# Gate-up biases as a 128-row fp32 table, chunk scores as 64x64 blocks, modulation rows turned by products with 36 moving columns

## What is computed

```
sh1, sc1, gt1, sh2, sc2, gt2 = split(silu(c) @ w_mod + b_mod)      # one row for the prompt, 8 for the samples
h  = rmsnorm(x) * (1 + sc1) + sh1
aq, af, ai, ag, bq, bk, bv, ga, gb = split(h @ w_in)
# HGRN2 branch, chunks of 64 tokens: inside a chunk
a = where(causal, einsum('bntha,bnsha->bnhts', q_dec, k_dec), 0)
# ... differential attention, merge, w_out, residual, second norm: h2
e1..e4 = top4(h2 @ w_router + b_router)                            # of 32 experts
gu = xb @ w_gate_up[e] + b_gate_up[e]                              # glu, lin = halves of 1024 columns
y  = ((clip(lin, -7, 7) + 1) * min(glu, 7) * sigmoid(1.702 * glu)) @ w_down[e] + b_down[e]
```

## Time and profile before

| | |
|---|---|
| runs | 1260.77, 1265.24, 1265.37 us |
| median | 1265.24 us |
| span of the profiled execution | 1258.5 us |
| TensorE products busy | 1102.0 us, 88% of the span |
| weight loads of TensorE / VectorE / ScalarE / GpSimd busy | 456.6 / 588.2 / 230.7 / 68.5 us |
| DMA | 485.30 MB, mean 386 GB/s |

### The profile page before, as it was taken

How to read it: one execution, slowest core, us unless ns; L and a number is a source line. 1 busy time by engine, 2 the same in 40 slices (tenths; PEclk the granted TensorE clock), 3 DMA queues, 4 the chain that set the end, 5 groups by cost and what they waited for, 6 DMA issues and landing times.

```text
span 1258.5 us, 23992 instructions
## 1 busy us (share of the span) xinstructions
PE 1102.0 (88%) x9856; PEld 456.6 (36%) x9856; DVE 588.2 (47%) x1166; ACT 230.7 (18%) x420; POOL 68.5 (5%) x126
## 2 busy tenths in 40 slices
PE   8999999999988697996887979999966995667996
PEld 4776777785322131321222322333211331112332
DVE  3536744444654252563353544666532552332654
ACT  3002510141311110220111211112100211100212
POOL 0312020250100000000000000000000000000000
PEclk9999999999989897998798999999988998888999
DMA  9979994599899999999999999999999999999995
GB/s 342 312 245 347 317 339 154 187 384 366 284 428 429 426 429 426 429 425 429 426 428 428 428 426 393 409 424 427 428 427 428 427 426 430 424 431 425 428 428 236
DMA packets 67619, 485.30 MB, mean 386 GB/s; under 512 B 6421, under 2 KB 29450, under 8 KB 40762
## 3 DMA queue, kind: packets, MB, share of 16 engines
q1 hardware_dynamic: 59312, 461.07, 88.9%
q0 software_dynamic: 7104, 19.65, 4.9%
q10 hardware_dynamic: 1130, 3.51, 0.8%
HBM read 479.47 MB, written 4.72 MB: 385 GB/s over the span
## 4 chain that ended last, share of the span: by engine, by line
DMA 45%; PE 27%; DVE 1%; issue 0%; DVEq 0%; ACT 0%; ACTq 0%
DMA big<-in_w_down 26%; PE PB L1247 13%; DMA big<-in_w_gate_up 13%; PE PB L1274 7%; DMA hTG<-in_w_down 5%; PE PB L1214 2%; PE PB L1201 2%; PE PB L1206 1%; PE PB L1229 1%; PE PB L1221 1%; PE PB L1240 0%; PE PB L1186 0%; PE PB L1232 0%; DVE big L1623 0%; DVE big L1620 0%
## 5 line engine op out<-in xcount | busy, mean ns | idle before, releaser
L1247 PE MATMUL PB<-big,cst 128*32 128x512 f32 x2768 | 355.0, 657 | 109.2 <-DMA big<-in_w_gate_up 109.2
L2189 DVE TENSOR_TENSOR tok<-PB,cst 32x512 f32<-32x512 f32 x188 | 129.1, 687 | 261.7 <-ACT cst L1554 259.8
L1247 PEld LDWEIGHTS PB<-big,cst 128*32 128x32 f32 x2768 | 89.0, 115 | 345.2 <-issue 181.1
L1274 PE MATMUL PB<-big,cst 128*32 128x512 f32 x1408 | 166.6, 602 | 12.8 <-DMA big<-in_w_down 12.7
L2165 DVE TENSOR_SCALAR mod<-PB 64x256 f32<-64x256 f32 x96 | 41.0, 427 | 209.1 <-PE PB L1247 208.4
L756 PE MATMUL PB<-hTG,big 128*128 128x264 f32 x576 | 136.5, 391 | 0.4 <-DVE hTG L1617 0.4
L756 PEld LDWEIGHTS PB<-hTG,big 128*128 128x128 f32 x576 | 106.9, 190 | 27.3 <-issue 10.8
L1544 ACT ACTIVATE mod<-PB 64x256 f32<-64x256 f32 x96 | 36.1, 376 | 422.3 <-PE PB L1247 421.7
L1274 PEld LDWEIGHTS PB<-big,cst 128*32 128x32 f32 x1408 | 39.2, 110 | 96.8 <-issue 65.8
L1201 PE MATMUL PB<-wide,att 128*32 128x256 f32 x784 | 57.9, 415 | 5.1 <-DVE att L2159 4.9
L1554 ACT ACTIVATE cst<-PB 128x512 f32<-128x512 f32 x48 | 28.7, 597 | 178.2 <-PE PB L1274 178.2
(11 more groups left out here) (378 smaller groups left out, 970.9 us busy)
## 6 DMA issues: line engine op xcount, KB each, us to landing
big<-in_w_gate_up SPq DMA_DIRECT2D x115, 2048.0 KB, 31.0
big<-in_w_down SPq DMA_DIRECT2D x57, 2048.0 KB, 23.9
hTG<-in_w_gate_up SPq DMA_DIRECT2D x13, 2048.0 KB, 37.1
big<-in_w_mod SPq DMA_DIRECT2D x24, 1024.0 KB, 7.5
big<-in_w_in SPq DMA_DIRECT2D x22, 1024.0 KB, 9.2
hTG<-in_w_down SPq DMA_DIRECT2D x6, 2048.0 KB, 24.0
wide<-in_cache_k POOLq DMA_DIRECT2D x16, 256.0 KB, 6.8
big<-in_w_out SPq DMA_DIRECT2D x4, 1024.0 KB, 10.5
```

The lines of the kernel that those rows point to most:

```text
L1247: mm = pe.matmul(GU[32 * j:32 * j + 32, :], mo["xT"][:, (2 * u + r) * M:(2 * u + r + 1) * M], groups(w[:, r * 2 * D:(r + 1) * 2 * D])[:, j ...
L1274: mm = pe.matmul(DN[32 * j:32 * j + 32, :], mo["actT"][:, (4 * u + r) * M:(4 * u + r + 1) * M], w[:, r * D + half * 512:r * D + (half + 1) ...
L2189: mm = dve.tensor_tensor(mo["y"][rows, :], DN[rows, :], mo["y_part"][other, :], ALU.add)
```

## The change

- biases becomes 128 rows of 512 fp32: rows 32j+e hold group j of expert e, filled by eight DMAs of the GpSimd queue with runs of 128 elements (512 bytes). VectorE adds 1 to rows 64 to 127 and signals biases_ready; the bf16 split, sel, and GpSimd's copy for it are gone.
- In `gate_up` each of the four bias products has a column of the fp32 identity, repeated 32 times, as stationary operand and the whole table as moving one. They stand ahead of the wait for xT_ready.
- Filler and clearing products read repeated zero rows in place of the biases tile; its clearing at the start is gone.
- `chunk_scores` makes two 64x64 products per head instead of one of 128x128.
- `first_cols` and `mod_cols` use an ordinary product of the same 128x128 stationary tile with the 36 useful columns of the identity; VectorE's reads follow.

```diff
@@ -189,8 +189,7 @@
         G = hTG[:, KC * T:KC * T + 2 * D].rearrange("p (s n) -> p s n", s=2)
         att_even = sb("att", [P, 2, 384])
         tok = sb("tok", [P, W])
-        biases = sb("biases", [96, 2 * D], BF16)
-        sel = sb("sel", [96, E], BF16)
+        biases = sb("biases", [P, 512])
         zeros_mask = sb("zeros", [P, P + NCH * E], BF16)
         zeros = zeros_mask[0:96, NCH * E:]
         small = sb("small", [P, 672])
@@ -210,6 +209,7 @@
             return cst[0:rows, at:at + w]
 
         ident = C("ident")
+        vector_rows = ident.rearrange("p (j r) -> p j r", j=4)[:, :, 0:9]
 
         def late_tile(i, n=H * T):
             return late[:, i * H * T:i * H * T + n]
@@ -262,8 +262,6 @@
         SH1p = late[:, 4 * SLOT:4 * SLOT + 256].rearrange("p (k r) -> p k r", k=KC)
         r4_rows = late[:, 4 * SLOT + 256:4 * SLOT + 768]
         b4_cols = late[:, 4 * SLOT + 768:4 * SLOT + 768 + 4 * 9].rearrange("p (j r) -> p j r", j=4)
-        bias_f = gates[0:E, 0:3 * D]
-        bias_t = gates[0:E, 3 * D:4 * D]
         wr = sb("wr", [P, KC, E])
         wrA = C("scan")[:, 0:KC * E].rearrange("p (k e) -> p k e", k=KC)
         br = sb("br", [P, E])
@@ -518,7 +516,11 @@
                 pool.dma_start(mod[32 * j:32 * j + 9, 1:3, :], src).then_inc(S("bmod_loaded"), 16)
             for i, n in enumerate(("lam_q1", "lam_k1", "lam_q2", "lam_k2")):
                 pool.dma_start(lamv[:, i, :], bass.AP(a[n].tensor, 0, [[0, P], [1, 64]])).then_inc(S("lam_loaded"), 16)
-            pool.dma_start(bias_f[:, 0:2 * D], a["b_gate_up"][0]).then_inc(S("bias_loaded"), 16)
+            for j in range(4):
+                src = a["b_gate_up"][0].rearrange("e (t u h j c) -> e t j h u c", t=2, u=2, h=2, j=2)[:, j // 2, j % 2]
+                dst = biases[32 * j:32 * j + 32, :].rearrange("e (h u c) -> e h u c", h=2, u=2)
+                for h in range(2):
+                    pool.dma_start(dst[:, h], src[:, h]).then_inc(S("bias_loaded"), 16)
             for j in range(4):
                 g = a["g_post_mix"] if j < 2 else a["g_post_ffn"]
                 src = bass.AP(g.tensor, (j % 2) * 512, [[0, 32], [1, 512]])
@@ -609,8 +611,6 @@
             for j in range(4):
                 pool.dma_start(own_cols_of(x_spill, j), own_rows(sx1, j)).then_inc(S("x_spilled"), 16)
 
-            pool.wait_ge(S("cst_loaded"), 16)
-            pool.tensor_copy(sel[:, :], C("onehot_e", 96)).then_inc(S("sel_ready"), 1)
             pool.wait_ge(S("h2_ready"), NCH)
             pool.wait_ge(S("x_spilled"), 16 * 4)
             pool.wait_ge(S("aux_full"), AUX["rt1"] + 1)
@@ -638,10 +638,14 @@
             def tr(out, in_, n=P):
                 return pe.transpose(out, in_, ident[0:n, 0:n])
 
+            def no_rows(n):
+
+                return zeros[:, 0:n // 4].unsqueeze(1).to_broadcast([96, 4, n // 4])
+
             def idle_products(n):
 
                 for _ in range(n):
-                    pe.matmul(PB[3][:, :], zeros[:, :], biases[:, 0:512], start=True, stop=True)
+                    pe.matmul(PB[3][:, :], zeros[:, :], no_rows(512), start=True, stop=True)
 
             pe.wait_ge(S("zeros_ready"), 1)
             idle_products(6)
@@ -687,7 +691,8 @@
                 pe.wait_ge(S("mod_free" if kind == 0 else "sc_rows"), 1)
                 bank = begin(name)
                 for q in range(2):
-                    mm = tr(bank[:, q * P:(q + 1) * P], mod[:, 0, kind * 256 + q * P:kind * 256 + (q + 1) * P])
+                    mm = pe.matmul(bank[:, q * 36:(q + 1) * 36], mod[:, 0, kind * 256 + q * P:kind * 256 + (q + 1) * P],
+                                   vector_rows, start=True, stop=True)
                 full(mm)
 
             def first_unit_shift():
@@ -731,7 +736,8 @@
                 pe.wait_ge(S("mod_free"), g + 1)
                 bank = begin(name)
                 for q in range(4):
-                    mm = tr(bank[:, q * P:(q + 1) * P], mod[:, g, q * P:(q + 1) * P])
+                    mm = pe.matmul(bank[:, q * 36:(q + 1) * 36], mod[:, g, q * P:(q + 1) * P], vector_rows,
+                                   start=True, stop=True)
                 full(mm)
 
             def proj_bank(name):
@@ -807,8 +813,11 @@
                 bank = begin(f"as{c}")
                 pe.wait_ge(S("hg_qk"), 1)
                 for h in range(H):
-                    mm = pe.matmul(bank[:, h * P:(h + 1) * P], KD[:, h, c * P:(c + 1) * P],
-                                   AQ[:, h, c * P:(c + 1) * P], start=True, stop=True)
+                    for i in range(2):
+                        cols = slice(c * P + i * CHUNK, c * P + (i + 1) * CHUNK)
+                        at = h * P + i * CHUNK
+                        mm = pe.matmul(bank[CHUNK * i:CHUNK * (i + 1), at:at + CHUNK], KD[:, h, cols], AQ[:, h, cols],
+                                       start=True, stop=True)
                 full(mm)
 
             def chunk_update(c):
@@ -1122,12 +1131,12 @@
                 full(pe.matmul(bank[:, 0:E], lparts[:, c, :], C("onehot_e"), start=True, stop=True))
 
             def zero(bank, n):
-                pe.matmul(bank[:, 0:n], zeros[:, :], biases[:, 0:n], start=True, stop=False)
+                pe.matmul(bank[:, 0:n], zeros[:, :], no_rows(n), start=True, stop=False)
 
             def add_zeros(n):
 
                 for _ in range(n):
-                    pe.matmul(acc(0, 0), zeros[:, :], biases[:, 0:512], start=False, stop=False)
+                    pe.matmul(acc(0, 0), zeros[:, :], no_rows(512), start=False, stop=False)
 
             out_samples()
             out_rows(0, 0, 0, 2)
@@ -1234,11 +1243,11 @@
                 mm.then_inc(S("gates_turned"), 1)
 
             def gate_up(e, b):
-                    pe.wait_ge(S("xT_ready"), b + 1)
                     pe.wait_ge(S("pgT_ready"), b + 1)
                     for j in range(4):
-                        pe.matmul(GU[32 * j:32 * j + 32, :], sel[:, e:e + 1].to_broadcast([96, M]), groups(biases[:, :])[:, j // 2, j % 2],
-                                  start=True, stop=False)
+                        pe.matmul(GU[32 * j:32 * j + 32, :], ident[:, 32 * j + e:32 * j + e + 1].to_broadcast([P, M]),
+                                  biases[:, :], start=True, stop=False)
+                    pe.wait_ge(S("xT_ready"), b + 1)
                     for u in range(4):
                         pe.wait_ge(*unit_landed(e * NU + u))
                         w = unit_slot(e * NU + u)
@@ -1282,7 +1291,7 @@
             gather()
             pe.wait_ge(S("aux_free"), AUX["rt1"] + 1)
             zero(ACC2, 256)
-            pe.wait_ge(S("sel_ready"), 3)
+            pe.wait_ge(S("biases_ready"), 1)
             blocks_of_first = pe.alloc_register("blocks_of_first")
             pe.reg_mov(blocks_of_first, 1)
             pe.wait_ge(S("samples_act"), 7)
@@ -1626,7 +1635,7 @@
                 do(dve.tensor_copy(out, in_), sem)
 
             do(dve.memset(zeros[:, :], 0.0))
-            do(dve.memset(biases[:, 0:512], 0.0), "zeros_ready")
+            dve.nop().then_inc(S("zeros_ready"), 1)
             do(dve.memset(small[:, :], 0.0))
             do(dve.memset(eps[:, :], EPS), "ssq_zero")
             do(dve.memset(cT[:, :, :], 0.0))
@@ -1667,13 +1676,13 @@
 
             def scale_cols(A, b4, kind, gains):
 
-                src = b4.rearrange("p (q j r) -> p j q r", q=4, j=4)[:, 2 * kind:2 * kind + 2, :, 0:9]
+                src = b4[:, 0:144].rearrange("p (q j r) -> p j q r", q=4, j=4)[:, 2 * kind:2 * kind + 2]
                 for j in range(2):
                     g = VT[:, gains + 4 * j:gains + 4 * j + 4].unsqueeze(2).to_broadcast([P, 4, 9])
                     stt(A[:, 4 * j:4 * j + 4, :], src[:, j], 1.0, g, ALU.add, ALU.mult)
 
             def shift_cols(SH, b4, kind):
-                src = b4.rearrange("p (q j r) -> p j q r", q=4, j=4)[:, 2 * kind:2 * kind + 2, :, 0:9]
+                src = b4[:, 0:144].rearrange("p (q j r) -> p j q r", q=4, j=4)[:, 2 * kind:2 * kind + 2]
                 for j in range(2):
                     copy(SH[:, 4 * j:4 * j + 4, :], src[:, j])
 
@@ -1681,7 +1690,7 @@
                 dve.nop().then_inc(S("aux_free"), 1)
 
             def by_group(b):
-                return b[:, 0:256].rearrange("p (q j r) -> p q j r", q=2, j=4)[:, :, :, 0:9]
+                return b[:, 0:72].rearrange("p (q j r) -> p q j r", q=2, j=4)
 
             dve.wait_ge(S("mod_used"), 4)
             copy(mod[:, 0, 256:512], PB[4][:, 0:256], "sc_rows")
@@ -1728,15 +1737,8 @@
                 do(dve.tensor_reduce(sv("lam", i, i + 1), lamv[:, 2 * i, :], AX, ALU.add))
             dve.nop().then_inc(S("lam_dots"), 1)
 
-            dve.wait_ge(S("bias_loaded"), 16)
-            ts(bias_f[:, D:2 * D], bias_f[:, D:2 * D], 1.0, None, ALU.add)
-            for i in range(2):
-                cols = slice(i * D, (i + 1) * D)
-                for part in range(3):
-                    copy(biases[32 * part:32 * part + 32, cols], bias_f[:, cols])
```

(5 more changed lines are left out.)

## The result

| | before | after |
|---|---|---|
| median, us | 1263.05 (20 runs, 1259.15 to 1329.51) | 1266.91 (20 runs, 1264.84 to 1273.43) |
| ratio after/before, 95% interval | | 1.0044 (1.0029 to 1.006) |
| span of the profiled execution, us | 1258.5 | 1263.4 |
| that execution's own time, us | not given | 1265.09 |

The ratio leaves the disturbed run of 1329.51 us out; on 1263.05 us it is +5.6 us (3.7 to 7.6), and the means of the 19 other runs before and the 20 after, 1262.7 and 1268.2 us, lie 5.5 us apart. The kernel became slower, but by less than the forecast's 7.8 us; 1266.91 us is, rounded, the lowest value of the range, and the ratio lies inside the 0.5% that counted as no change, with the interval across that border.

A forecast was written before the change was run, and what follows sets the result against it. TensorE's product list was taken to bound the kernel to about 340 us, the expert weight stream after that. Front stage +1.0 and expert stage +6.8 us on 1265.2 gave 1273.0 us, range 1267 to 1279.

The forecast's parts named there:

- Price of the group: Four bias products of each expert block: fp32 group 0.86 us for 0.22, so 0.64 us more TensorE time per block.
- rival 3: Expert blocks: bias products run two after two, not abreast; a group takes 1.7 us, 1285 us in all; chance 0.06.
- First block: Start of the expert stage: fp32 group starts 0.43 us sooner but lasts 0.64 us longer, +0.2 us on the path.
- Stall: Late slot release at 786.31 us, where the weight stream waits for TensorE: two more costly blocks, +1.3 us.
- Three experts: Two-block experts behind the 786.31 us release: period 30.30 us against 29.4 of DMA, 0.9 us each, +2.7 us (0 to 3.9).
- rival 1: Expert stage: queued weights cover the three experts, the tail pays only its last two groups; +3.8 us, 1269 us; chance 0.30.
- Tail: Last blocks, from 1157.11 us to the end: six bias groups less 1.2 us of waiting, +2.6 us (1.3 to 3.8).
- Part 2: Front stage, modulation rows by 36 columns: turned tiles go from 0.12 to 0.20 us, twelve tiles, +1.0 us (-1.0 to 1.4).
- Part 3: Front stage, chunk scores as 16 half-size instructions for 8: no change, ends for two calls -0.7 and +1.2 us.
- Part 4: Bias preparation at the start: fewer VectorE instructions, eight GpSimd DMA issues for one; priced at 0, ends -1.5 and +3.8 us.
- rival 4: Front stage: GpSimd's 3.8 us of later issues come through to the cached key pages; 1277 us; chance 0.06.
- The sum's base: Starting time of the whole-kernel sum: 1265.2 us, the median of runs, taken to stand 6.7 us over the profiled 1258.5 us span.

The follow-up runs named there:

- r1 to r3: Changed kernel with bf16 bias table, fp32 bias group issued twice in experts 15-19; 1-14 and 20-27; or 28-31: ratios 1.0086, 1.0037, 1.0068 to the kernel before.

## Why the prediction was right or wrong

**Bound and mechanism: right.** Two regimes, a stall at 780 to 790 us, a stream with 0.4 us to spare per two-block expert behind it, and an end set by TensorE. r1 to r3 show that the cost sits where the prediction put it and that 30 other blocks hide it.

**Price of the group: right.** 0.23 to 0.88 us in the first block; block periods 14.505 to 15.141 us, +0.636 for 0.64. The four products run abreast; rival 3 is out.

**First block:** +0.14 us for 0.2. The first block itself began at 336.27 us, and "a first block before 337 us" had been named as a sign of being wrong. It was a poor sign: 0.84 us of the 1.29 us by which it came sooner stand at the end of the start-up already (first input projection at 23.93 us for 24.77), and the rest is about the 0.43 us of the move.

**Stall:** +1.4 us for 1.3.

**Three experts:** 2.3 us for 2.7 (0.8 us each by the rates, for 0.9), between the bounds. Releases came every 30.28 us for 30.30. By the means of four profiles of each kind it is less, 3.0 - 1.4 = 1.6 us: this is the term of the expert stage that was sized too high, and with it the stage's 6.8 us, for which 5.5 us (5.2 in the means) were measured. The 29.4 us of DMA for an expert was from a mean rate; that units already queued hide the rest is likely but not shown. It is not 0 as in rival 1, whose mechanism is out although its 1269 us is nearer to what was measured.

**Won back:** the sum had no such term; the trace shows 0.76 us between the 34th block and 1157.63 us. In the means it is 0.3 us, and stages of equal kernels differ by more (920.4 to 922.3 us), so it is no more than scatter.

**Tail:** +2.61 us for 2.6 (2.5 in the means); the 1.2 us of waiting is used up.

**Part 2:** +1.2 us for 1.0: 0.23 us for each turned tile in `mod_cols`, near the upper value of 0.24. The two fp32 instructions of a tile go at the pace of a transpose each, so the product with fewer columns is the dearer one.

**Part 3: mis-sized.** -0.6 us for 0, near the end of -0.7. The interpolation by columns between 0.04 and 0.10 us gave 0.06; the instructions with 64 stationary columns, whose outputs alternate between two halves, went as fast as those with 32. Whether the alternation does it or such a load is as cheap anyway, no run separates. The Trainium skill (TensorE: Matmul & The Clock Gate, LDWEIGHTS) would give 53 ns a load, an estimate of 0.85 us a call; the trace has 0.62 us for 16, 39 ns. The measurement decides, for a figure below both.

**Part 4: VectorE right, GpSimd open.** VectorE's 14 instructions are gone and the copy behind them, 2.0 us earlier, waits for TensorE as before, so nothing was gained on the path. Timeline of DVE, kernel after, which answers to the earlier trace rows:

```profile
53.27 0.42 DVE L1626 TENSOR_SCALAR biases<-biases 64x512 f32<-64x512 f32 x1
...
64.74 0.68 DVE L1635 COPY big<-PB 8x512 f32<-8x512 f32 x1 [11.05 <-PE PB L639]
```

11 us of idle time took their place, as forecast, with TensorE as the releaser. GpSimd's eight issues took 4.35 us for one's 0.54, and the last early key page was issued at 52.10 us, 3.5 us later. Timeline of POOL:

```profile
41.01 4.35 POOL L523 DMA_DIRECT2D biases<-in_b_gate_up  x8
...
52.10 0.54 POOL L543 DMA_DIRECT2D wide<-in_cache_k  x1 [0.51 <-issue]
```

The first use of a key page was at 86.25 us, before 86.86: that cover held. What may not be free is the wait near 106 us, in which the prediction saw nothing of the table. It is no more than a microsecond on average, so rival 4's 3.8 us is out.

**The sum's base: the step that failed.** "The median of the runs stands 6.7 us over the profiled span" was read as a fixed distance. It is 1.7 us in every profiled execution whose time is known; the other 5 us are the distance between the two groups of runs, for which the runs point at the start-up. Two of the three runs shown lay in the upper group, and the profile, by its quick start, in the lower one. Of the 6.1 us between 1273.0 and 1266.9, 3.5 us is this base (1265.24 to 1261.77, the median without the run of 1329.51 us), and the other 2.6 us are that by these medians the change cost 5.1 us and not 7.8. Part of that is again the groups: nine of the 19 runs of the kernel before lay in its upper group, and seven of 20 of the kernel after. With the groups compared each with its like it is 6.5 us, with fillers on both sides 7.3, against 7.8. From the profiled execution itself the sum is 1258.5 + 1.7 + 7.8 = 1268.0 us, against 1266.1 for the lower group of the kernel after.

That the measured median reaches the range at all is partly luck. It stands on the lowest value of a range centred 6 us higher. That value was set for rival 1 with some scatter, and rival 1 did not come true: the base and the term of the three experts were off in the same direction.

**Chances.** Slower by over 0.5% had 0.60 and within 0.5% 0.36. The ratio came out at 1.0044, its interval on both sides. A cost of about 5 to 7 us lies just at the 0.5% line of this kernel, so the forecast had too much confidence for its distance of 1.5 us from that line.

## What to carry to other kernels

An extra TensorE cost per block is paid only where slot releases come later than the stream wants them: set the block period times the blocks of one refill against the DMA time of that refill, and count only the blocks where the first is larger, and those after the last landing. Compare two profiles from one landmark on, such as the first product of a stage, before their spans are subtracted; and look at the single runs for groups before a median of three is taken as the base. An fp32 product with few moving columns is no cheap stand-in for a transpose (two instructions against one), while halving both operands of a product whose off-diagonal blocks are thrown away does pay, 0.3 us a call in the traces here and too little for the runs to show.

## What the runs showed of the hardware that was not expected

- An fp32 instruction with 64 stationary and 64 moving columns, outputs alternating between two halves, takes 0.039 us (16 in 0.62 us). Its row lasts 0.69 us for 16, just as that of 16 instructions with 32 columns does, and not in between them and the 0.10 us of 128 columns.
- At the start the same products take 1.94 or 1.07 us for 16, and the transposes 3.35 or 2.16 us for 12, in different executions of like code; three of 14 profiles stay at the slow pace until past 25 us. That puts the first block at 341.6 to 346.2 us for 336.2 to 340.2. The profile's own row of the granted clock shows 1.00 in both cases. Fillers in the gaps narrowed twelve runs to 1258.8 to 1260.9 us, beside 1258.3 to 1266.2.
- A share of DMA near 1.0 does not say that the stream is full: from 845 to 860 us it was 1.01 at 425 GB/s before and 0.99 at 402 GB/s after.
